# Inverse roots as exp(-log(x)/2) on ScalarE, and the convolution stage rearranged, in a two-block transformer kernel

## The reference, cut to what matters

```python
def rms_norm(x, g):
    y = xf * lax.rsqrt(jnp.mean(xf * xf, axis=-1, keepdims=True) + EPS)
    return (y * g).astype(x.dtype)

def conv_mixers(h, w_in, conv_a_w, conv_a_b, ln_a_g, ln_a_b, conv_b_w, w_out):
    a_val, a_gate, b_gate, c_gate, b_val = jnp.split(h @ w_in, ...)
    a = a_val * jax.nn.sigmoid(a_gate)
    a = causal_depthwise_conv(a, conv_a_w) + conv_a_b          # 31 taps
    a = jax.nn.silu(group_layer_norm(a, 8 groups of 64, ln_a_g, ln_a_b))
    bb = b_gate * causal_depthwise_conv(c_gate * b_val, conv_b_w)   # 3 taps
    return jnp.concatenate([a, bb], axis=-1) @ w_out
```

## Time and profile before

| | |
|---|---|
| median of 3 runs | 2411.84 us (2411.57 to 2415.27) |
| the profiled execution: its own time | 2407.98 us |
| its span | 2406.1 us, mean granted clock 0.971 |
| TensorE matmuls busy | 2254.8 us, 94% of the span |
| VectorE | 1537.6 us, 64% |
| ScalarE | 1077.2 us, 45% |
| GpSimd | 813.6 us, 34% |
| convolution stage, first slab to first matmul of `mix` | 1572.8 to 1660.8 us |

### The profile page before, as it was taken

The page is one execution under the profiler, slowest core; times in us unless marked ns, Lnnn a source line. Parts: engine busy times, 40 slices in busy tenths (PEclk is TensorE's granted clock), DMA queues, the critical chain, the costliest instruction groups (busy, mean ns, idle before and its releaser), DMA issues.

```text
span 2406.1 us, 41252 instructions
## 1 busy us (share of the span) xinstructions
PE 2254.8 (94%) x16556; PEld 2089.2 (87%) x16556; DVE 1537.6 (64%) x2647; ACT 1077.2 (45%) x1983; POOL 813.6 (34%) x738
## 2 busy tenths in 40 slices
PE   6999999899989999999799899997999999888998
PEld 5878679889987787699799899987899999887997
DVE  5866567598777765686898764377644644437443
ACT  4554322455446453323555544414544544445443
POOL 2441102136435531121255243244442343132441
PEclk9999899999999998999999999998999999999999
DMA  6773248546765742386367655643456556533554
GB/s 223 199 196 103 94 169 300 185 147 214 251 227 152 215 134 84 134 293 241 132 219 247 209 169 183 185 138 116 163 186 179 172 184 182 164 123 132 184 180 127
DMA packets 121949, 429.27 MB, mean 178 GB/s; under 512 B 14959, under 2 KB 16927, under 8 KB 121632
## 3 DMA queue, kind: packets, MB, share of 16 engines
q1 hardware_dynamic: 94208, 333.80, 41.8%
q0 software_dynamic: 27408, 91.77, 13.1%
q10 hardware_dynamic: 144, 1.07, 0.1%
HBM read 425.48 MB, written 1.10 MB: 177 GB/s over the span
## 4 chain that ended last, share of the span: by engine, by line
PE 84%; DVE 10%; ACT 4%; issue 2%; POOL 0%; DMA 0%; SPq 0%; DVEq 0%; ACTq 0%
PE bank L375 21%; PE bank L377 21%; PE bank L376 20%; PE bank L740 5%; PE bank L365 3%; PE bank L463 2%; DVE u L1544 2%; DVE ring_lo L1556 2%; PE bank L440 1%; DVE std L1580 1%; PE bank L455 1%; PE bank L557 1%; PE bank L394 1%; ACT ring_hi L885 1%; PE bank L599 1%
## 5 line engine op out<-in xcount | busy, mean ns | idle before, releaser
L375 PE MATMUL bank<-x_hi,ring_hi 128*128 128x256 f32 (+2 forms) x3040 | 885.2, 291 | 47.5 <-DVE x_lo L2194 13.9
L1556 DVE TENSOR_TENSOR ring_lo<-ring,ring_hi 128x1024 fp32r<-128x1024 f32 (+1 forms) x436 | 585.3, 1344 | 486.1 <-ACT ring_hi L885 485.9
L376 PE MATMUL bank<-x_lo,ring_hi 128*128 128x256 f32 (+2 forms) x3040 | 873.8, 287 | 0.0
L377 PE MATMUL bank<-x_hi,ring_lo 128*128 128x256 f32 (+2 forms) x3040 | 873.4, 287 | 0.0
L885 ACT ACTIVATE ring_hi<-ring 128x1024 fp32r<-128x1024 f32 (+1 forms) x550 | 567.2, 1034 | 327.4 <-PE bank L377 245.5
L2311 POOL TENSOR_TENSOR ring_lo<-ring,ring_hi 128x1024 fp32r<-128x1024 f32 (+1 forms) x156 | 398.4, 2554 | 773.8 <-ACT ring_hi L885 497.6
L375 PEld LDWEIGHTS bank<-x_hi,ring_hi 128*128 128x128 f32 x3040 | 584.2, 192 | 67.2 <-issue 28.8
L377 PEld LDWEIGHTS bank<-x_hi,ring_lo 128*128 128x128 f32 x3040 | 584.8, 192 | 0.0
L376 PEld LDWEIGHTS bank<-x_lo,ring_hi 128*128 128x128 f32 x3040 | 583.2, 192 | 0.5
L377 PE MATMUL bank<-hid_hi,ring_lo 128*128 128x256 f32 (+1 forms) x1056 | 299.8, 284 | 0.0
L375 PE MATMUL bank<-hid_hi,ring_hi 128*128 128x256 f32 (+1 forms) x1056 | 298.6, 283 | 0.0
(11 more groups left out here) (316 smaller groups left out, 2932.7 us busy)
## 6 DMA issues: line engine op xcount, KB each, us to landing
ring<-in_w_gu SPq DMA_DIRECT2D x192, 512.0 KB, 3.5
ada_ring<-in_ada POOLq DMA_DIRECT2D x144, 512.0 KB, 5.0
ring<-in_w_in SPq DMA_DIRECT2D x136, 512.0 KB, 4.4
ring<-in_ffn_up SPq DMA_DIRECT2D x104, 512.0 KB, 3.5
ring<-in_w_down SPq DMA_DIRECT2D x64, 512.0 KB, 3.5
ring<-in_w_branch SPq DMA_DIRECT2D x32, 512.0 KB, 4.3
ring<-in_ffn_down SPq DMA_DIRECT2D x32, 512.0 KB, 5.0
ring<-in_w_down SPq DMA_DIRECT2D x32, 384.0 KB, 3.3
```

Source lines behind the costliest of these rows:

```text
L375: pe.matmul(b[:, cs], ring_hi[:, i_hi, c0], x1, start=first and k == 0, stop=False)
L376: pe.matmul(b[:, cs], ring_hi[:, i_hi, c0], x2, start=False, stop=False)
L377: m = pe.matmul(b[:, cs], ring_lo[:, i, c0], x1, start=False, stop=last and k == nk - 1)
L1556: dve.tensor_tensor(ring_lo[:, i, 0:cols], ring[:, i, 0:cols], ring_hi[:, n % HIGH, 0:cols].bitcast(f32), ALU.subtract).then_inc(split(n)[ ...
```

## The change

Three things are changed.

1. Every inverse root is made on ScalarE in two activations, Ln and then Exp with scale -0.5, in the place of Sqrt on ScalarE and reciprocal on VectorE. The bank is free for TensorE after the Ln ("log"). The calls of `use_tables(Sqrt)` become `use_tables(Ln)` or are left out, and several of `use_tables(Exp)` are left out.
2. The slabs of the convolution stage come in another order (`CONV_ORDER`): the value and gate slabs of the four tiles stand early, the others between them. `ca` has four tiles' room, `cb` and `bu` two each.
3. The layer norm goes tile by tile while the slabs are still being used: the two partial sums of the taps are added and centred in one step by two matmuls with the matrix `centre` (identity minus group mean), ScalarE squares, one matmul gives the variance, Ln and Exp the inverse root. The output product `mix` takes its first four slabs in parts, over banks 4 to 7: rows 4, 5, 6 first, then 7, then 0 to 3; slabs 4 to 7 go as before.

```diff
+CONV_ORDER = [(0, 0), (0, 1), (1, 0), (1, 1), (0, 2), (0, 3), (2, 0), (2, 1), (0, 4), (1, 2), (3, 0), (3, 1), (1, 3), (1, 4)]
+CONV_ORDER += [(j, k) for j in (2, 3) for k in (2, 3, 4)]
...
             def low_root(b, i, name, dim):
                 act.wait_ge(*at(pe_, "norm", *name))
-                act.activation(low_stat[i], bank[b][:, 0:T], ACT.Sqrt, scale=1.0 / dim, bias=eps_ap).then_inc(*sig(act_, "std", *name))
+                act.activation(low_stat[i], bank[b][:, 0:T], ACT.Ln, scale=1.0 / dim, bias=eps_ap).then_inc(*sig(act_, "log", *name))
+                act.wait_ge(*at(act_, "log", *name))
+                act.activation(low_stat[i], low_stat[i], ACT.Exp, scale=-0.5).then_inc(*sig(act_, "inverse", *name))
...
-                act.activation(std[:, i, cs], bank[b][:, cs], ACT.Sqrt, scale=1.0 / dim, bias=eps_ap).then_inc(*sig(act_, "std", *name))
+                act.activation(std[:, i, cs], bank[b][:, cs], ACT.Ln, scale=1.0 / dim, bias=eps_ap).then_inc(*sig(act_, "log", *name))
+                act.wait_ge(*at(act_, "log", *name))
+                act.activation(std[:, i, cs], std[:, i, cs], ACT.Exp, scale=-0.5).then_inc(*sig(act_, "inverse", *name))
...
-                use_tables(ACT.Sqrt)
                 latent_squares(l)
                 root_a(l, 0)
                 root_a(l, 1)
...
                 low_root(7, 1, ("kvlat", l), 128)
-                use_tables(ACT.Exp)
...
                 decay_logs(l, 1)
-                use_tables(ACT.Exp)
+                use_tables(ACT.Ln)
...
                     if hd == 1:
-                        use_tables(ACT.Sqrt)
                         root_b(l, 0, 0)
                         root_b(l, 0, 1)
...
                         root_b(l, 1, 1)
-                        use_tables(ACT.Exp)
...
-            def recip(i, name, cs=ALL):
-                dve.wait_ge(*at(act_, "std", *name))
-                dve.reciprocal(std[:, i, cs], std[:, i, cs]).then_inc(*sig(dve_, "recip", *name))
-                dve.wait_ge(*at(dve_, "recip", *name))
+            def inverse_root(i, name, cs=ALL):
+                dve.wait_ge(*at(act_, "inverse", *name))
                 return std[:, i, cs]
...
             def mix_out(layer):
+                whole = range(KD)
+                if layer == 0:
+                    for j in range(4):
+                        begin(("mix", 0, j))
+                        claim(slab_bank(("mix", 0, j)), dve_, "xm", 0, j)
+                        mix_part(j, (4, 5, 6), True, False)
+                    for j in range(4):
+                        mix_part(j, (7,), False, False)
+                    for j in range(4):
+                        mix_part(j, (0, 1, 2, 3), False, True)
+                    whole = range(4, KD)
...
+            def centred(j):
+                b = claim(2 + j % 2, dve_, "ln", j)
+                pe.wait_ge(*at(dve_, "tap", j, 30))
+                for i, x in enumerate(taps_of(j)):
+                    m = pe.matmul(b[:, 0:N2], cc("centre"), x, start=i == 0, stop=i == 1)
+                m.then_inc(*sig(pe_, "centred", j))
...
             def conv_mixers():
+                for n, (j, k) in enumerate(CONV_ORDER):
+                    project_raw(("conv", j, k) if k < 4 else ("convg", j), u, TEXT, (act_, by[k], j), None if n else first)
+                    if (j, k) in ((2, 1), (3, 0), (2, 2), (3, 2)):
+                        centred({(2, 1): 0, (3, 0): 1, (2, 2): 2, (3, 2): 3}[j, k])
+                    if (j, k) in ((1, 2), (1, 3), (2, 3), (3, 3)):
+                        variance({(1, 2): 0, (1, 3): 1, (2, 3): 2, (3, 3): 3}[j, k])
```

More of the change, by code:

```diff
@@ L1452, in mix_out, with evict @@
                     if j == KD - 1:
-                        use_tables(ACT.Sqrt)
+                        use_tables(ACT.Ln)
                     square_x(3 * layer + 2, j, dve_, "xm", layer, j)
             def conv_mixers():
+                def evict(name, to, done, f, *free):
+                    halves(name)
+                    act.wait_ge(*used(name))
+                    if free:
+                        act.wait_ge(*at(*free))
+                    act.activation(to, bank[slab_bank(name)][:, 0:N2], f).then_inc(*sig(act_, *done))
@@ L1476, in conv_mixers @@
-                for j in range(4):
-                    halves(("convg", j))
-                    act.wait_ge(*used(("convg", j)))
-                    act.activation(bg[:, j, :], bank[slab_bank(("convg", j))][:, 0:N2], ACT.Copy).then_inc(*sig(act_, "bg", j))
-                use_tables(ACT.Sqrt)
-                for j in range(4):
-                    act.wait_ge(*at(dve_, "centred", j))
-                    act.activation(s_sb[:, j, 0:N2], y[:, j, 0:N2], ACT.Square).then_inc(*sig(act_, "ln_sq", j))
@@ new lines, in conv_mixers @@
+                a_pair(0)
+                a_pair(1)
+                c_gate(0)
+                b_value(0)
+                a_pair(2)
+                squared(0)
+                b_gate(0)
+                c_gate(1)
+                evict(("conv", 3, 0), ca[:, 3, HA:], ("a", 3), ACT.Copy)
+                squared(1)
+                evict(("conv", 3, 1), bg[:, 3, :], ("a_gate", 3), ACT.Sigmoid)
+                use_tables(ACT.Ln)
+                ln_root(0)
+                b_value(1)
+                ln_root(1)
@@ new lines, in conv_mixers @@
+                b_gate(1)
+                c_gate(2)
+                squared(2)
+                mixed_high(0, 4, pool_, "ybg", 0)
+                b_value(2)
+                ln_root(2)
+                b_gate(2)
+                mixed_high(0, 5, pool_, "ybg", 1)
+                c_gate(3)
+                squared(3)
+                halves(("conv", 3, 3))
+                b_value(3)
+                halves(("convg", 3))
+                ln_root(3)
+                use_tables(ACT.Silu)
+                mixed_high(0, 6, pool_, "ybg", 2)
@@ L1492, in moba_pair @@
+                for j in range(3):
+                    ln_silu(j)
+                b_gate(3)
+                halves(("mix", 0, 0))
+                for j in range(3):
+                    mixed_high(0, j, act_, "ln_silu", j)
+                mixed_high(0, 7, pool_, "ybg", 3)
+                ln_silu(3)
+                mixed_high(0, 3, act_, "ln_silu", 3)
             def moba_pair(i):
@@ L1679, in latent_norms @@
             def latent_norms(l):
-                for i, name in enumerate((("qlat", l), ("kvlat", l))):
-                    dve.wait_ge(*at(act_, "std", *name))
-                    dve.reciprocal(low_stat[i], low_stat[i]).then_inc(*sig(dve_, "recip", *name))
-                dve.wait_ge(*at(dve_, "recip", "kvlat", l))
+                dve.wait_ge(*at(act_, "inverse", "kvlat", l))
                 for x in range(2):
```

233 lines of the change are left out of this document (122 added, 111 removed).

## The result

The changed kernel takes 2451.2 us (median of 4 runs, 2448.65 to 2455.26), the kernel before 2412.57 beside it (4 runs, 2411.57 to 2415.27): ratio 1.016, 95% interval 1.0141 to 1.0179. It is slower by 38.6 us. The forecast was 2431 with a range up to 2444: the sign was right, but the sum of the forecast was +20.7, 17.9 short. The profiled execution of the changed kernel is the slowest of its four, 2455.26 with a span of 2453.5 and a mean granted clock of 0.962, against 2407.98 and 0.971 before; sums over the two profiles therefore come to 47.4 and not to 38.6.

A forecast was written before the change was run, and what follows sets the result against it. TensorE, 84% of the chain, was taken as the bound. The terms -0.8 + 19.1 + 10.7 + 3.6 - 3.0 - 8.9 = +20.7 gave 2428.7 from the profiled 2407.98, 2432.5 from the median; forecast 2431, range 2418 to 2444.

The forecast's parts named there:

- Which table holds what: ScalarE's roots: the table taken for Ln has no Exp, so each new root is Ln, load, Exp.
- A single root: Each of 15 chain roots at sublayer boundaries: 2.23 to 2.32 us before, 2.19 after; -0.8 us in all.
- The six roots in the mixers: Attention A and latents: loads in ScalarE's queue delay `chunk_states` by 10.0 us in layer 0, 9.1 in layer 1; +19.1 us.
- The four roots of B: Attention B in the mixers: `latent_v` waits for bank 7 and starts 5.4 us later per layer; +10.7 us.
- Roots at the boundaries, starts, loads left out: Chain roots -0.8 us, six SwiGLU and feed-forward starts +3.6, Exp loads left out near layer starts -3.0.
- The convolution stage: New slab order, tile-by-tile layer norm and `mix` in parts end the last slab at 1676.6, not 1685.5; -8.9 us.
- Four slabs at 2.83: 1676.6: End of `mix`: after the parts at 1665.3, the last four slabs follow at 2.83 us each and end at 1676.6.
- the 8.3 us of parts and phases: In `mix`: 12 matmuls of slab 3 and phases 7 and 0 to 3 take 8.3 us from 1657.1.
- GpSimd starved: New convolution stage: GpSimd's products are held by VectorE's taps, so the stage gains 4 us at most: 2436; chance 0.14.
- TensorE isn't held in the mixers: TensorE does other work until bank 7 is free, so the 30 us fall to a few: 2407 to 2414; chance 0.08.
- the rival's sum was -34: All roots: Ln and Exp share one table, no load between them, so -34 us to 2378; chance 0.06.

The follow-up runs named there:

- The kernel with Sqrt in the mixers: The whole change, but the 20 roots and 4 latent roots in the mixers go back to Sqrt and reciprocal: 2413.58 us.
- the one with the stage alone: The kernel before with only the new convolution stage added, every root still Sqrt and reciprocal: 2411.39 us, ratio 0.999.
- with the loop broken: ScalarE makes slab j+4's high part before tile j's next-sublayer input: 2402.2 us on the one with the stage alone, 2383.74 on the run with one table.
- the run with one table: The whole change, but the table set holding both Ln and Exp is loaded by name in place of the dummy Lns: 2390.05 us, ratio 0.9907.

## Why the prediction was off

The forecast had the mechanism: loads between Ln and Exp keep bank 7 from TensorE in the mixers, and it sized those waits well. Two of its steps failed. It priced the six roots by the wait alone and left the lower clock behind the wait in the bounds, and it let the last four slabs of `mix` follow at TensorE's own pace.

- **Which table holds what**: right. 31 + 4 + 4 loads at the Exps, as forecast.
- **A single root**: right. In the changed kernel, one at 1925.72 gives its Exp at 1927.93, 2.21 us, forecast 2.19:

```profile
1925.72 0.48 ACT L940 ACTIVATE std<-bank,small 128x256 f32<-128x256 f32 x1 [2.25 <-PE bank L440]
1926.21 1.28 ACT L942 ACT_TABLE_LOAD   x1
1927.51 0.42 ACT L942 ACTIVATE std<-std 128x256 f32<-128x256 f32 x1
1927.94 1.28 ACT L913 ACT_TABLE_LOAD   x1
1929.34 1.99 ACT L920 ACTIVATE ring_hi<-ring 128x1024 fp32r<-128x1024 f32 x2
```

- **The six roots in the mixers**: the wait was right to 0.2 us in both layers (10.2 and 9.2 with the clock kept up, forecast 10.0 and 9.1). This step failed in what it left out, the price of the lower clock behind the wait. It put "+22 if TensorE also starts slowly after the long wait" into the bounds and took 19.1, the waits alone; measured 26.5, and filling the wait gave 6 to 8 back. With waits of 2.35 and 5.90 us (2.36 and 6.33 in layer 1) the granted clock was 1.2 GHz from 207.7 to 224.8 in layer 0, and for as long in layer 1, 9.9 and 10.4 us of it behind the waits, and for 6.8 us once more from 231.6 and 938.1; a fall, of 6.8 us at 190.6 in layer 0, already delayed the roots by 2.0. Before, with no wait over 0.7 us, it fell for 3.4 to 6.8 us at a time in this place.
- **The four roots of B**: right, 11.1 for 10.7, and 5.4 and 5.6 a layer in the trace for 5.4.
- **Roots at the boundaries, starts, loads left out**: -0.2 was forecast for the three together. The kernel with Sqrt in the mixers less the one with the stage alone gives 2413.58 - 2411.39 = +2.2 by the medians and +3.1 by the ratios. It holds the stage's four roots as well, and the two intervals leave about 3 us either way, so it isn't clear of -0.2. The fence above shows why starts cost: load and Exp go ahead of two high parts, for which GpSimd's split of the next slab waits. At the first SwiGLU start behind the stage TensorE waits 1.56 us for that split, at 1737.47; the offset rises by 1.7 there and gives 0.8 back within 7 us. No run measures the starts apart.
- **The convolution stage**: the step that failed is "Four slabs at 2.83: 1676.6". All before it held, to the 8.3 us of parts and phases, which took 9.8 as the clock fell for 3.4 us in them. (The 8.3 is 69 matmuls at 0.12: nine of slab 3's, not the twelve that the prediction names.) After the parts, which ended at 1708.1, the last four slabs took until 1723.5, 1682.3 of the old clock: 15.4 us for 11.3, with one wait of 1.80 for an addition in the loop and one more fall of the clock. So the stage's shortfall is in the loop and in the clock, and neither was a term. Term by runs, which have Sqrt in the stage: -1.0 for -8.9 (-2.4 by the ratio), and -9.8 with the loop broken (-9.4), which holds the 1.74 us of SwiGLU too.
- **GpSimd starved** (rival): its product of tile 2 did take 6.69 us, but the waits for row 6 and for slab 3 ended within 0.3 us of where the forecast without starvation had them.
- **TensorE isn't held in the mixers** (rival): false, both waits are in the trace.

The sizes as measured are 26.5 + 11.1 + 2.2 - 1.0 = 38.8. That this meets the 38.6 confirms nothing: the four are steps of one chain of medians, from the change to the kernel before, and must add up to its ends. Of the 18 missing, 7.4 are in the first term (the clock), 0.4 in B's, 2.4 in the boundaries, and 7.9 in the stage (the loop and the clock).

Open: why the run with one table stands at -22.4 where the rival's sum was -34. With the loop broken it is -28.3; of these 5.9, 3.1 stand at the loop in the profiles. The rest was not taken apart. Open too are 2.8 us that the profile of the stage alone lost between 1720 and 2220, in code that it shares with the kernel before: the clock fell there at 2104.6 and 2203.6, and in the kernel before at neither.

## What to carry to other kernels

A function pair that looks like one operation can cost two table loads each time: count the loads in the trace between the two, and either name the set that has both or do all of the first function before the second, which was worth 61 us (the set named, for all the roots) and 36 to 38 (the order, in the mixers alone) here. Price a wait of TensorE with what follows it: its own length, and the stretch at the lower clock behind it, which the busy share doesn't show. When work is made to finish in a bunch, look for the loop of engines that consumes it: if one tile's round trip is longer than the bunch's spacing, start the part that depends on nothing first. And when single runs are taken out of a change one after another, their differences add up to the whole whatever the causes are; only the traces tell whether each one is what it is called.

## What the runs showed of the hardware that was not expected

A set loaded by name stays for every activation that it serves: the kernel with one table does 33 loads, the change 96, and none of the 33 stands inside a root. The two largest groups:

```profile
L913 ACT ACT_TABLE_LOAD x10 | 12.8, 1283 | 0.2
L1472 ACT ACT_TABLE_LOAD x4 | 5.1, 1283 | 0.1
```

A wait of TensorE can cost more than its own length: with 17 matmuls a layer whose result nobody reads, put into 8 us of waiting, the clock stayed at 2.4 GHz, and the median fell by 8.4 us. And 3.4 us at 1.2 GHz cost 1.3 to 1.6 us each time they fell into a dense stretch; where they fall differs between kernels whose code is the same there, which is one reason why two profiles differ by more than two medians.
